# Two-layer hybrid encoder trunk on one core: first head's K copied on ScalarE, weights split in another order, last head's output kept on chip, W_o tile 0 split ahead, last row tile in halves

## What is computed

```python
for i in range(DEPTH):                      # DEPTH = 2
    if i % 2 == 0:
        mix = diff_attention(x, w_qkv, w_o, lam_vec, subln_g, lambda_init)     # 8 heads of 128
    else:
        mix = neighborhood_attention(x, w_qkv, b_qkv, rpb, w_o, b_o)           # 16 heads of 64, 8 x 16 window
    x = layer_norm(alpha * x + mix, ln_g[i, 0], ln_b[i, 0])
    ff = conv_ffn(x, w_in, b_in, conv_w, conv_b, w_out, b_out)                 # 1024 -> 2 x 2816 -> 1024
    x = layer_norm(alpha * x + ff, ln_g[i, 1], ln_b[i, 1])
```

## Time and profile before

| | before |
|---|---|
| median of 3 executions (lowest to highest) | 2799.16 us (2797.43 to 4436.93) |
| profiled execution | 2802.47 us |
| its span | 2800.5 us |
| TensorE busy, of the span | 95% |
| VectorE, POOL, ScalarE busy | 69%, 60%, 43% |
| granted TensorE clock, mean | 0.978 |

### The profile page before, as it was taken

The page is one execution under the profiler, slowest core; times in us unless marked ns, Lnnn a source line. Parts: engine busy times, 40 slices in busy tenths (PEclk is TensorE's granted clock), DMA queues, the critical chain, the costliest instruction groups (busy, mean ns, idle before and its releaser), DMA issues. The chain is left out here.

```text
span 2800.5 us, 35855 instructions
## 1 busy us (share of the span) xinstructions
PE 2658.3 (95%) x13043; PEld 2220.2 (79%) x13043; DVE 1927.1 (69%) x2479; ACT 1191.7 (43%) x1785; POOL 1671.4 (60%) x1179
## 2 busy tenths in 40 slices
PE   8999999988899999999989999998788999999998
PEld 6788888877778888888868888887677888888886
DVE  3766667683677766677774777777477777666768
ACT  3455444552253333333344555555415333333333
POOL 4444444333487667777744666655457776677775
PEclk9999999998999999999999999998899999999999
DMA  3010000235011112121222212211411211121212
GB/s 121 21 31 30 30 28 22 64 94 186 15 56 46 46 61 60 46 61 46 63 95 54 56 48 50 47 46 53 156 39 55 60 46 46 59 62 46 60 46 91
DMA packets 214044, 163.83 MB, mean 58 GB/s; under 512 B 36283, under 2 KB 195595, under 8 KB 213899
## 3 DMA queue, kind: packets, MB, share of 16 engines
q1 hardware_dynamic: 213755, 161.38, 19.5%
q10 hardware_dynamic: 144, 0.52, 0.1%
HBM read 137.24 MB, written 24.64 MB: 58 GB/s over the span
## 5 line engine op out<-in xcount | busy, mean ns | idle before, releaser
L1400 POOL TENSOR_TENSOR ff_Rlf<-raw_weights 128x512 f32<-128x512 f32 x210 | 330.6, 1587 | 53.4 <-PE ff_ph L1497 32.6
L1407 POOL TENSOR_TENSOR ff_Rl<-ff_Rlf,ff_Rh 128x512 fp32r<-128x512 f32 x210 | 310.7, 1496 | 25.2 <-ACT ff_Rh L1663 25.2
L1407 POOL TENSOR_TENSOR ff_Rl<-raw_weights,ff_Rh 128x512 fp32r<-128x512 f32 x84 | 157.8, 1888 | 253.5 <-ACT ff_Rh L1663 253.5
L1663 ACT ACTIVATE ff_Rh<-ff_Rlf 128x512 fp32r<-128x512 f32 x210 | 130.5, 630 | 366.6 <-POOL ff_Rlf L1400 366.4
L1497 PE MATMUL ff_ph<-XTh,ff_Rh 128*128 128x512 f32 x672 | 263.2, 392 | 8.7 <-POOL ff_Rl L1407 8.4
L1497 PE MATMUL ff_ph<-XTl,ff_Rh 128*128 128x512 f32 x672 | 262.2, 390 | 0.0
L1497 PE MATMUL ff_ph<-XTh,ff_Rl 128*128 128x512 f32 x672 | 262.1, 390 | 0.0
L1544 PE MATMUL ff_po<-ff_WDh,WH 128*128 128x512 f32 x624 | 244.5, 392 | 0.0
L1544 PE MATMUL ff_po<-ff_WDh,WL 128*128 128x512 f32 x624 | 243.0, 389 | 0.0
L1544 PE MATMUL ff_po<-ff_WDl,WH 128*128 128x512 f32 x624 | 242.9, 389 | 0.0
L1765 DVE TENSOR_TENSOR X<-ff_po,X 128x512 f32<-128x512 f32 x288 | 191.4, 684 | 66.0 <-PE ff_po L1544 66.0
(11 more groups left out here) (330 smaller groups left out, 7457.6 us busy)
## 6 DMA issues: line engine op xcount, KB each, us to landing
raw_weights<-in_ffn_w_in SPq DMA_DIRECT2D x168, 256.0 KB, 3.3
ff_WDlf<-in_ffn_w_out SPq DMA_DIRECT2D x40, 512.0 KB, 4.0
raw_weights<-in_attn_w_qkv SPq DMA_DIRECT2D x24, 512.0 KB, 3.7
raw_weights<-in_na_w_qkv SPq DMA_DIRECT2D x24, 512.0 KB, 4.2
rpb_rows<-da_rows SPq DMA_DIRECT2D x2, 3840.0 KB, 26.7
na_B<-rpb_rows SPq DMA_DIRECT2D x32, 224.0 KB, 4.4
wo_oraw<-heads_t SPq DMA_DIRECT2D x12, 512.0 KB, 4.6
da_E<-in_x SPq DMA_DIRECT2D x8, 512.0 KB, 6.6
```

What stands on the lines that cost most here:

```text
L1400: nc.gpsimd.tensor_tensor(out=Rf[:, i % SLOTS], in0=quad(*a), in1=quad(*b), op=op).then_inc(quad_sum, 1)
L1407: nc.gpsimd.tensor_tensor(out=Rl[:, i % SLOTS], in0=src, in1=Rh[:, i % SLOTS].bitcast(F32), op=ALU.subtract).then_inc(quad_low, 1)
L1663: nc.scalar.activation(Rh[:, i % SLOTS], src, ACT.Copy).then_inc(quad_high, 1)
```

## The change

Five edits. (1) In the first projection half of the first head the 24 matmuls go by product, not by slot, and the waits are spread: `wh` and the copied x at the start, `x_low` before the second eight, `w_low` before the third. (2) POOL's `double_k(0)` goes away; ScalarE copies KH instead (`first_double`), once before and once behind its read of the last projection half; POOL does `split(1, 0)` ahead of the first head's K, and `split(1, 1)` when VectorE has finished KL. (3) The last head's output is written by VectorE to `tail`, a buffer on chip over XTl slot 6; it is neither stored nor loaded, and the stage's end no longer waits for such stores. (4) W_o tile 0 is split during the last head into slot 5 of XTh and XTl (`weight_high` on ScalarE; `weight_low` on VectorE in the first attention, on POOL in the second), the output stage's first 24 matmuls read it there, and later both parts are copied to WH and WL; ScalarE and VectorE split `tail` into slot 7 at the start. (5) In the last layer's end tile 4 is finished with tile 5 behind tile 6's variance, and tile 7 is finished and stored in two halves. In the first layer the order of the finishes is as before. Places without an edit in the text below are as they were.

```diff
 class FirstHeads:
+    def weight_high(self, act):
+        self.prefetch.wait(act)
+        self.nc.scalar.activation(self.XTh[:, WEIGHT_SLOT], self.weights, ACT.Copy).then_inc(self.weight_rounded, 1)
+
+    def weight_low(self, eng, engine):
+        eng.wait_ge(self.weight_rounded, 1)
+        engine.tensor_tensor(out=self.XTl[:, WEIGHT_SLOT], in0=self.weights, in1=self.XTh[:, WEIGHT_SLOT].bitcast(F32),
+                             op=ALU.subtract).then_inc(self.weight_split, 1)
...
 # diff_attention_stage, SP
-            head(H - 1, False, False, False)
-            store(H - 1, 2)
-            store(H - 1, 3)
+            head(H - 1, False, False, False, last=True)
             prefetch.wait(sp)
             for b in range(2):
-                sp.wait_ge(o_stored[b], 16 * 2 * H)
+                sp.wait_ge(o_stored[b], 16 * 2 * (H - 1))
...
 # diff_attention_stage, POOL
             for j in range(3):
                 split(0, j)
-            double_k(0, (const_set, 2))
-            for j in range(2):
-                split(1, j)
+            split(1, 0)
+            pool.wait_ge(kl_dup, 2)
+            split(1, 1)
...
 # diff_attention_stage, TensorE, project
                 if i0 == 0:
-                    if j % 2 == 0:
+                    if isinstance(h, int) and h == 0 and j == 0:
+                        pe.wait_ge(w_high, 1)
+                    elif j % 2 == 0:
                         pe.wait_ge(w_low, 3 * h + j // 2 + 1)
...
+                by_part = isinstance(h, int) and h == 0 and j == 0
                 for i in range(i0, i0 + n):
-                    k, p = i // 3, i % 3
+                    k, p = (i % KT, i // KT) if by_part else (i // 3, i % 3)
+                    if by_part and i == KT:
+                        pe.wait_ge(x_low, QT // 2)
+                    if by_part and i == 2 * KT:
+                        pe.wait_ge(w_low, 1)
...
-            pe.wait_ge(x_low, QT // 2)
+            pe.wait_ge(x_high, QT // 2)
             project(0, 0, 0, 3 * KT)
...
 # diff_attention_stage, ScalarE
+            def first_double(c):
+                a, b = slice(c * DH, (c + 1) * DH), slice((1 - c) * DH, (2 - c) * DH)
+                act.wait_ge(stack_high, 2 * c + 1)
+                nc.scalar.activation(KH[b, c], KH[a, c].bitcast(F32), ACT.Copy).then_inc(kh_dup, 1)
...
             stacks(0, False)
+            first_double(0)
             for j in ORDER[5:]:
                 take(0, j)
+            first_double(1)
...
                 ready.high(act, 1)
+                ready.weight_high(act)
                 late_o(o + 3)
...
 # diff_attention_stage, VectorE
                 late_map(QT - 1)
+                ready.weight_low(dve, nc.vector)
                 finish_o(h, 2, late_bank(o + 2))
...
 # Norm and SpreadNorm: half a finish
+    def finish_half(self, dve, t, half):
+        dve.wait_ge(self.gained, t + 1)
+        dve.wait_ge(self.rooted, t + 1)
+        at = slice(half * BANK, (half + 1) * BANK)
+        self.nc.vector.scalar_tensor_tensor(out=self.X[:, t, at], in0=self.gained_at[t % 4][:, at], scalar=self.rstd[:, t:t + 1],
+                                            in1=self.gb[:, 1, at], op0=ALU.mult, op1=ALU.add).then_inc(self.finished_y, 1)
...
 # output_stage, SP
             for k in range(2, KT):
-                if k == 2:
-                    sp.wait_ge(first_low, 1)
-                else:
+                if k > 2:
                     sp.wait_ge(w_low, k - 2)
                 sp.dma_start(raw[:, k % 2], w_o[k * P:(k + 1) * P, :]).then_inc(w_in[k % 2], 16)
-                if k >= READY_HEADS + 2:
+                if READY_HEADS + 2 <= k < KT - 1:
                     sp.wait_ge(o_low, k - READY_HEADS - 1)
                     load_head(k)
...
 # output_stage, POOL
             for k in range(1, KT):
-                pool.wait_ge(w_high, k + 1)
+                pool.wait_ge(w_high, k)
                 nc.gpsimd.tensor_tensor(out=wl[:, k], in0=raw[:, k % 2], in1=wh[:, k].bitcast(F32),
                                         op=ALU.subtract).then_inc(w_low, 1)
+                if k == 2:
+                    nc.gpsimd.tensor_scalar(wl[:, 0], XTl[:, WEIGHT_SLOT].bitcast(F32), 1.0, 1.0, ALU.mult,
+                                            ALU.mult).then_inc(first_copied, 1)
...
 # output_stage, TensorE
+                high, low = (XTh[:, WEIGHT_SLOT], XTl[:, WEIGHT_SLOT]) if k == 0 and t < FIRST else (wh[:, k], wl[:, k])
...
             for k in range(KT):
-                if k == 0:
-                    pe.wait_ge(first_low, 1)
-                else:
+                if k:
                     pe.wait_ge(w_low, k)
...
 # output_stage, ScalarE
-            for k in range(KT):
+            for k in range(1, KT):
                 if k >= 2:
                     act.wait_ge(w_in[k % 2], 16 * (k // 2))
                 nc.scalar.activation(wh[:, k], raw[:, k % 2], ACT.Copy).then_inc(w_high, 1)
+                if k == 1:
+                    nc.scalar.activation(XTh[:, KT - 1], tail[:], ACT.Copy).then_inc(tail_high, 1)
+                    nc.scalar.activation(wh[:, 0], XTh[:, WEIGHT_SLOT].bitcast(F32), ACT.Copy).then_inc(first_copied, 1)
...
 # ffn_stage
+        ENDS = {t: [] for t in range(TT)} | ({6: [4, 5], 7: [6, 7]} if last_layer else {5: [4], 6: [5], 7: [6, 7]})
...
 # neighbourhood_stage, SP: no stores of head H - 1; POOL, ScalarE and VectorE:
-                sp.wait_ge(o_stored[i], 16 * 2 * H)
+                sp.wait_ge(o_stored[i], 16 * 2 * (H - 1))
...
+                    if s == 10 and h + 1 == H:
+                        ready.weight_low(pool, nc.gpsimd)
...
+                    if s == 9 and h + 1 == H:
+                        ready.weight_high(act)
...
+                if h + 1 == H:
+                    place = tail[(q // 2) * DH:(q // 2 + 1) * DH, (q % 2) * BANK + at:(q % 2) * BANK + at + 2 * P]
```

More of the change, by code:

```diff
@@ L24 @@
 READY_HEADS = 2
+WEIGHT_SLOT = 5
+TAIL_SLOT = 6
 def hold(eng, sem, value, passed):
@@ L85, with __init__ @@
 class FirstHeads:
-    def __init__(self, nc, m, raw, OT, XTh, XTl, tiles):
+    def __init__(self, nc, m, raw, OT, XTh, XTl, tiles, weights, prefetch):
+        self.weights, self.prefetch = weights, prefetch
+        self.weight_rounded, self.weight_split = m.sem("weight_rounded"), m.sem("weight_split")
         self.nc, self.raw, self.OT, self.XTh, self.XTl, self.tiles = nc, raw, OT, XTh, XTl, tiles
@@ L178, in diff_attention_stage @@
         LAST = H - 1
-        ready = FirstHeads(nc, m, raw, OT, XTh, XTl, READY_HEADS)
+        ready = FirstHeads(nc, m, raw, OT, XTh, XTl, READY_HEADS, shared_raw[:, 0], prefetch)
         late_v = [x[:, KT - 1].rearrange("p (k n) -> p k n", n=P) for x in (XTh, XTl)]
@@ L269, in head @@
                     load(h + 2, 2)
-                store(h, 0)
+                if not last:
+                    store(h, 0)
                 if load_three_on:
                     load(h + 3, 1)
-                store(h, 1)
+                if not last:
+                    store(h, 1)
             for j in range(3):
@@ L1918, in _ @@
                 norm.variance(dve, t)
-                if t - 1 in FINISHED:
-                    norm.finish(dve, t - 1)
-                if t == TT - 1:
-                    norm.finish(dve, t)
+                for u in ENDS[t]:
+                    if u < TT - 1 or not last_layer:
+                        norm.finish(dve, u)
+                    else:
+                        for half in range(2):
+                            norm.finish_half(dve, u, half)
                 if t >= 4 and not last_layer:
```

82 lines of the change are left out of this document (52 added, 30 removed).

## The result

The changed kernel takes 2774.78 us (median of 4 runs, 2772.56 to 2777.88), the kernel before beside it 2799.01 us (2797.43 to 4436.93): ratio 0.9909, 95% interval 0.9897 to 0.9922, which is 24.2 us less by the medians. The forecast was 2776.0 us, within 2767 to 2786. The profiled execution took 2774.96 us with a span of 2773.2 us, 27.3 us less than the span before: 3.1 us more than the medians give, mostly because the profiled run of the kernel before (2802.47 us) was 3.5 us above its median, and that of the changed kernel only 0.2 us above.

What follows compares the result with a forecast made beforehand. TensorE, busy 95% of the span, bounds the kernel; gains come where it waits or runs at half clock. 9.3 + 4.5 + 7.5 + 1.9 = 23.2 us off the 2799.16 us median gives 2776.0 us, range 2767 to 2786.

Steps and rivals of the forecast that it cites:

- start of the first attention: First projections to POOL's first scaling: shorter weight waits and less half clock, less late splits; 9.3 us won.
- end of the first attention: First output stage: no wait for the last store or tile 0's split; first matmul 4.5 us earlier.
- end of the second attention: Second output stage: TensorE starts 8.7 us earlier, less 0.8 for the clock and 0.4 for POOL's subtraction; 7.5 us.
- end: Last layer's end: tile 7's sums and finishes 1.3 us earlier, halved last store 0.6 us; 1.9 us won.
- whether so short a gap lets the clock fall the trace answers once: First projection: one 1.80 us gap had a clock fall; bounds 2.4 (falls) and 4.8 us (stays), 3.8 taken.
- The bound of 11.2: Start of the first attention: the most that could be won, 11.2 us, with the clock held.
- I take the same length again, so nothing: First output stage: half clock after the start lasts 5.8 us as before, so the clock gains nothing.
- The bias load only delays tile 1: 3.2: Second output stage: the 3.2 us issue makes tile 1 ready 6.7 us after the start, inside tile 0's 7.7.
- Costs nothing: Output stage: tile 0's copies ahead of tile 2's operands cost nothing, as these are needed 13 us after the start.
- the start keeps its wait: Rival, first attention's start: clock falls, VectorE's K stack or POOL's late splits replace the wait; 4 us, 2781.3; chance 0.14.
- a stage's end stays as late: Rival, attention ends: another transfer SP awaits ends as late; 2.2 and some 2.8 us lost, 2781.0; chance 0.06.
- Slower by half clock: Rival, output stages' first four row tiles: TensorE stays at half clock; 2857.6 us, slower by 2.1%; chance 0.02.

Runs made afterwards that it cites:

- tile0_late: Full change, but W_o tile 0 is copied and subtracted at the output stage's start, as in the kernel before: 2781.35 us, ratio 0.9928 to the kernel before.
- copy_early: Full change, but POOL makes split(1, 1)'s copy early and waits for VectorE's K stack only ahead of the subtraction: 2774.49 us, ratio 0.9905 to the kernel before.
- bias_behind: Kernel before, but ScalarE issues the second output stage's bias load behind its copy of W_o tile 1: 2797.25 us, ratio 0.999.
- weights_first: Full change, but tile 2's weights load ahead of heads 2 and 3, the bias load behind head 3's copy: 2773.58 us, ratio 0.9899 to the kernel before.

## Why the prediction was right

The time came out 1.2 us below the forecast, by its mechanism. That it is so close is in part luck: term by term the marks give 27.3 us, 4.1 more than the forecast's 23.2, and 3.1 of these are not in the medians. Four terms are right to within about 1 us; what they leave out is mostly clock, which comes and goes between executions. From the marks:

| term | forecast (bounds) | measured |
|---|---|---|
| start of the first attention | 9.3 (8.3 to 11.2) | 10.3 |
| end of the first attention | 4.5 (2.2 to 6.0) | 4.4, and 1.3 by the clock |
| end of the second attention | 7.5 (5 to 9) | 6.9 = 8.73 - 1.58 behind the start - 0.25 in the last head |
| end | 1.9 (0.5 to 2.6) | 2.0 |
| elsewhere | 0 | 2.3 |

- *Start.* The scores came at 52.05, not 53.1. The step that was off is "whether so short a gap lets the clock fall the trace answers once", by which I gave the clock 1.4 of its 2.4 us. One row for that was too few (last section). Another 0.3 us is not the edit's: the first weights landed earlier, so POOL's copy began at 10.85 and not at 11.11. The bound of 11.2 does not come out of the steps either: with the clock held they give 11.0. VectorE's stack at its minima, ScalarE's order and the 0.7 us for POOL's late splits (11.0 less 10.3) came as forecast.
- *End of the first attention.* 1.14 us behind the last write, as by the earlier trace rows, and `tile0_late` shows the other part, 2.35 us of split. "I take the same length again, so nothing" was the weak step for the clock: it was back 3.0 us after the start, not 5.8; half of the difference is 1.4 us, and the marks give 1.3.
- *End of the second attention.* 8.7 us is what the marks show. Of the 1.6 us lost behind it, 0.9 are the restart (4.8 us at half clock against 3.0, forecast 0.8) and 0.4 the wait at tile 2; 0.3 is not explained. POOL's subtraction stretched VectorE's sum by 0.16 us (0.58 against 0.42), not by 0.4, but delayed POOL's own scaling to 1950.15; the last head lost 0.25 us in all. "The bias load only delays tile 1: 3.2" was wrong in size: it took 0.38. "Costs nothing" for tile 2 was wrong by 0.43 us, because I counted when it is needed, not when three transfers of 0.5 MB and the bias load would land, nor that VectorE's and POOL's subtractions would meet there.
- *End.* 1.5 us by the order of the finishes and 0.5 by the halved last store (from the last finish's end to the span's end 3.35 us, before 3.87), as forecast.
- *Elsewhere.* The three clock stretches named here add up to 1.6 of the 2.3 us: in the last values (1.6 us won), behind a gap of 3.11 us at 821.82 in the first feed-forward stage before but not after (1.7 won), and behind one of 3.15 us at 2138.62 in the second one after but not before (1.7 lost).

Of the rivals, *the start keeps its wait* and *a stage's end stays as late* fell with the first marks. *Slower by half clock* had no share: TensorE was back at full clock 3.0 and 4.8 us after the two starts.

## What to carry to other kernels

Count a wait at a stage's start as a sum of separate queues: 9.8 us between the last write and the first matmul were a barrier of 1.0, a store's landing of 2.9, one DMA issue of 3.2 us ahead of ScalarE's first copy, and a copy and subtraction of 2.6. Each of the last three goes by its own edit, and the cheapest is to move the issue. Where two engines hinder each other, put into the gap the piece that is over before the other engine begins, and look at who waits for the piece that is pushed back. In `copy_early` that was POOL's copy (43.42 to 44.47, VectorE's stack from 44.99). That it is a copy does not make it harmless. In the kernel before, a subtraction of VectorE (alone 1.22 us) had no work of POOL beside it but the two copies of KH. It took 1.95 us, and the copies 1.97 and 1.69, where POOL's copy of a whole tile takes 1.05:

```profile
49.93 1.97 POOL L344 TENSOR_SCALAR da_KH<-da_KH 64x1024 fp32r<-64x1024 f32 x1 [26.73 <-ACT da_KH L657]
```

```profile
51.02 1.95 DVE L761 TENSOR_TENSOR da_QS<-da_raw,da_QS 64x1024 fp32r<-64x1024 f32 x1
```

A gain below 2 us can be read from marks close to the edit; the medians of a few runs don't show it, and marks far behind it don't either, since one stretch of half clock between them is worth 1.7 us.

## What the runs showed of the hardware

- The clock's fall behind a short gap is not settled by the gap. The same gap of 1.80 us ahead of the last values stands in all fourteen profiles; in five the clock was at half within 1.3 us, in nine it was not. Of one where it fell, `copy_early`:

```profile
628.00:630.00 2.00, 1.73 (x12) 1.74 (x13) 1.33 (x2) 0.85 (x1) 2.00 (x3) 0.85 0.00 0
630.00:632.00 2.00, 2.00 (x11) 2.00 (x11) 1.80 (x1) 0.00 (x0) 0.72 (x1) 0.50 0.00 0
```

  Here the stretch lasted 3.4 us at 1.2 GHz (629.4 to 632.8), which costs 1.7 us. What else decides is open; no run varied it alone.
- One DMA issue of the same 0.5 MB broadcast took 3.20, 3.19, 2.97, 2.76, 1.98, 1.79 and 0.38 us on ScalarE's queue, the last in all eight kernels where W_o tile 0 was split ahead. Neither a store under way nor the place in the queue explains this alone (`tile0_late`, `bias_behind`); the cause is open.
- The first load that SP issued in an output stage of `weights_first` was in use 3.6 and 4.4 us after the stage's beginning (first and second stage). The third load, in the full change, was in use after 6.8 us, and in the second stage, with the bias beside it, after 9.1 us.
